# One tile's tables, attention and projections rearranged in a two-block transformer kernel

## The chip, the cores and the metric

The kernel runs on one core of a Trainium2 chip. Its time is the device time of one execution, in microseconds (us). Engines are named as in the profile: PE (TensorE), DVE (VectorE), ACT (ScalarE), POOL (GpSimd), SP (SyncE, which here only issues transfers). Everything is float32.

## The reference, cut to what matters

Sequence 256, width 1024, 16 meta tokens in front. Two blocks follow each other. The first is a mixer and an expert layer:

```python
proj = rms_norm(h, norm1_g) @ w_in
attn = sliding_window_attention(q, k, v, ...)      # head norms of q and k, window 128, sinks, 8 heads
ssm  = s5_ssm(u, ...)                              # 32 groups, 64 complex states, gelu, gate
h = h + concat(rms_norm(attn), rms_norm(ssm)) @ w_out
q = rms_norm(h) @ w_query                          # 8 product-key heads, top 16 of 16384 experts each
h = h + sum over 8*16 experts of gelu(peer_u[idx] . h) * g * peer_v[idx]
```

The second block has an "even" layer (dilated and differential attention) and an "odd" layer (MoBA and NSA attention), each of the form

```python
p = rmsnorm(x, ln) @ w_in          # 8 column chunks: heads, values, gates
x = x + concat(attention_a * silu(gate_0), attention_b * silu(gate_1)) @ w_out
```

## The kernel before, in words

The tokens are cut into two tiles of 128, T = 0 and T = 1 (the meta tokens go with tile 0). The program is written out by hand: each stage is a generator for each engine which emits some instructions and yields, and `steps`, `side_by_side`, `beside`, `paced` and `woven` (lines 219 to 258 and 2038) weave generators into one order. Every engine runs its own instructions in the order in which they were emitted and waits on semaphores. A round is one such yield.

**Mixer, tile 0 (up to about 145 us).** `Tables` (line 688) makes sines and cosines of 16 x 145 angles: DVE makes the angles of the first half (`angles`), ACT the sines (`first_sines`), POOL folds the output matrices (`pool`, line 787, seven operations of 128x512) and then makes the angles of the second half (three operations of 128x1160), and ACT takes an absolute value and the second sines (`last_sines`). Then `ssm(t, 0)` (56 rounds, three for each of 16 steps j and a tail: PE drives, DVE rotates, scans and turns back, PE reads out) is run `beside` a second lane `mixer`, which gets 0.8 rounds for each round of the scan: `project_u`, then `norm1(1)` with `project_qkv(0)`, `last_sines`, `head_norm1(0)` with `project_u1`, `attention1(0)` with `project_qkv(1)`, `mix_attention(0)`. After it come `close_mixer(0)` side by side with `head_norm1(1)`, and half of `query(0)`.

**Expert layer (about 165 to 990 us).** `Peer` gathers 256 times 128 rows of 8 KB (line 1387; 16 experts x 8 heads x 2 tiles) through POOL's queue into 6, then 7, then 8 buffers. In each round n DVE takes the dot products (line 1320), ACT the gelu, the weight and a diagonal matrix (lines 1354 to 1361), and PE two matmuls of two passes each (line 1374), which free the buffer; a quarter of tile 1's rows are added on DVE (line 1300) instead. The first 32 gathers use 6 buffers, since the seventh lies over tile 1's attention data; the rest wait for `attn_ready[1]`. One step of the lane `rest` is emitted per round: the rest of `query(0)`, `attention1(1)` (one head per step; one PSUM bank for turned probabilities, `turn_bank`), `mix_attention(1)`, `ssm(1)`, `close_mixer(1)`, `query(1)`. After round 140 two steps of the second block's tile 0 lane (`ahead`) are added per round.

**Second block.** `Lane` holds a tile's buffers and banks. `project` (line 1649) multiplies eight chunks of weights, 16 matmul instructions each (line 1681), into `banks`: one bank (`pa`), or two where `L.spare` is set (tile 0, until the gathers end). Its generator for ACT evicts each chunk in the round in which PE's last matmul of it was emitted (lines 1704 to 1728). `stream` is the attention. Tile 1's lane (`main`) starts when the gathers are done and runs beside what is left of tile 0's odd layer, which stops before its compression step until `L.done["far"]` is set there. A lane that has sent its output sets `L.done["finished"]`.

**Weights.** A ring of three buffers is filled by SP in the order of use (line 127), a chunk as soon as the chunk three before it is used.

Of the kernel before, what the change touches and what calls it, by code (L numbers as in the profile page):

```python
# [267 lines left out]
def norm1(t, T):  # L268
# [34 lines left out]
    def dve():  # L303
        t.dve.wait_ge(t.constants, 32)
# [124 lines left out]
def head_norm1(t, T):  # L429
# [4 lines left out]
    n = 2 if T == 0 else 1  # L434

# [17 lines left out]
    def dve():  # L453
# [19 lines left out]
        t.dve.tensor_scalar(t.QTt[T][:, :, :], t.PS[2][:, :].rearrange("p (a m) -> p a m", a=4), t.col("qn"), -0.125,  # L473
                            ALU.mult, ALU.mult).then_inc(*placed.add())
        t.dve.wait_ge(*turned.at(2))
        t.dve.tensor_scalar(t.KTt[:, :, T * P:(T + 1) * P], t.PS[3][:, 0:2 * P].rearrange("p (g m) -> p g m", g=2),
                            t.col("kn"), None, ALU.mult).then_inc(*placed.add())
        if T == 0:
            t.dve.tensor_scalar(t.KTt[:, :, SEQ:],
                                t.PS[3][:, 2 * P:2 * P + 2 * META].rearrange("p (g m) -> p g m", g=2),  # L480
                                t.col("kn"), None, ALU.mult).then_inc(*placed.add())
# [3 lines left out]
    def pe():  # L485
# [4 lines left out]
        if T == 1:  # L490
            t.pe.wait_ge(*t.half_added[0])
        for a in range(4):
            ins = t.pe.transpose(t.PS[2][:, a * P:(a + 1) * P], t.qx[:, a * P:(a + 1) * P], t.ident[:, :])
        ins.then_inc(*turned.add())
        t.pe.wait_ge(*normed.at(n + 2))
        for g in range(2):
            ins = t.pe.transpose(t.PS[3][:, g * P:(g + 1) * P], t.kx[:, g].rearrange("p x d -> p (x d)"), t.ident[:, :])
        if T == 0:
            t.pe.wait_ge(*normed.at(n + 3))
            for g in range(2):  # L500
                ins = t.pe.transpose(t.PS[3][:, 2 * P + g * META:2 * P + (g + 1) * META],
# [7 lines left out]
def attention1(t, T):  # L509
# [15 lines left out]
    turn_bank, out, apt = t.PS[2], t.PS[3], t.apt[T]  # L525

    def pe():
# [16 lines left out]
        def turn(i):  # L544
            t.pe.wait_ge(*expd.at(i + 1))
            if i >= 1:
                t.pe.wait_ge(*placed.at(i))
            for e in range(E):
                c = 0
                for n, (k0, k1) in enumerate(kb):  # L550
                    m = (e * (n_k + 1) + n) * P
                    ins = t.pe.transpose(turn_bank[0:k1 - k0, m:m + P], p_at(i, e)[:, c:c + k1 - k0], t.ident[:, :])
                    c += k1 - k0
# [14 lines left out]
        for i in range(NU + 4):  # L568
            if i < NU:
                scores(i)  # L570
            if i >= 4:
                mix(i - 4)
            if 2 <= i <= NU + 1:
                turn(i - 2)
            yield

    def dve():
# [4 lines left out]
        for i in range(NU + 4):  # L582
            if i < NU:
                t.dve.wait_ge(*scored.at(i + 1))
                if i >= R:
                    t.dve.wait_ge(*turned.at(i - R + 1))
                for e, h in enumerate(sets[i]):
                    ins = t.dve.tensor_tensor_reduce(p_at(i, e), s_at(i, e), bias, 1.0, t.nsink[:, h:h + 1], ALU.add,  # L588
                                                     ALU.min, t.amn[:, h:h + 1])
                ins.then_inc(*least.add())  # L590
            if i == NU:
# [13 lines left out]
    def act():  # L605
        for i in range(NU + 4):
            if 3 <= i <= NU + 2:
                n = i - 3
# [3 lines left out]
                of = turn_bank[:, 0:E * (n_k + 1) * P].rearrange("p (e n m) -> p e n m", e=E, m=P)  # L612
# [3 lines left out]
            if 1 <= i <= NU:  # L616
                n = i - 1
# [6 lines left out]
            if i == NU + 1:  # L624
# [63 lines left out]
class Tables:  # L688

    HALF = ST // 2

    def __init__(self, t):
# [4 lines left out]
        self.dts, self.turns, self.sines, self.folded = (t.sem(x) for x in ("t_dts", "t_turns", "t_sines", "t_folded"))  # L699
        t.diagonal, t.folded, t.sines = self.dts.at(3), self.folded.at(1), [self.sines.at(2), self.sines.at(3)]  # L700
# [31 lines left out]
    def angles(self):  # L732

        t, ch = self.t, self.t.dch
        h = slice(0, self.HALF)
        S, C = t.SIN[:, h, :], t.COS[:, h, :]
        ch.step(t.dve.tensor_tensor(S, bc(self.frac[:, h], SPAN + 1), bm(t.col("time"), self.HALF), ALU.mult))
        ch.step(t.dve.tensor_scalar(C, S, ROUND, ROUND, ALU.add, ALU.subtract))
        ch.step(t.dve.tensor_tensor(S, S, C, ALU.subtract))
# [1938 lines left out]
```

## Time and profile before

| | us |
|---|---|
| median of three executions (1281.91 to 1285.24) | 1283.33 |
| the profiled execution: its own time | 1284.34 |
| its span, from first to last instruction | 1282.6 |
| busy PE / DVE / ACT / POOL | 1103.5 / 758.7 / 528.1 / 319.8 |
| first and last gather issued (line 1387) | 164.7, 975.9 |
| tile 0's and tile 1's outputs sent (line 2388), first and last | 1096.1, 1280.3 |

A busy share is an average over stages with different limits, so the profile is read stage by stage. An "x" with a number counts instructions; "idle before" is the engine's idle time ahead of a group, with what ended it.

### The profile page before, as it was taken

The numbers are of one execution on the slowest core, as the hardware profiler recorded it, in microseconds if no ns is written. First come the engines' busy times: TensorE is split into PE (matmuls) and PEld (weight loads), VectorE is DVE, ScalarE is ACT, GpSimd is POOL, SyncE is SP. The second block draws the span as 40 slices with busy tenths as digits, with TensorE's granted clock in tenths as the row PEclk, the third lists the DMA queues.
The fourth block names the chain that finished last, engine by engine and source line by source line (L and its number), as shares of the span: only waits on it lengthen the run. The fifth ranks groups of instructions, "written<-read, shape, count | busy, mean of one in ns | idle before, by whom it ended". The sixth has DMA issues, their size and how long they took to land.

```text
span 1282.6 us, 12167 instructions
## 1 busy us (share of the span) xinstructions
PE 1103.5 (86%) x3770; PEld 585.4 (46%) x3770; DVE 758.7 (59%) x1973; ACT 528.1 (41%) x1381; POOL 319.8 (25%) x302
## 2 busy tenths in 40 slices
PE   5998778888999979986898969898887899988998
PEld 5675534434444434432343434343432644543675
DVE  6564463469999666468775777785566322332343
ACT  4332226844344544344556463555463221212231
POOL 5100022244444333334232234333223000000000
PEclk9989889999999999999899999999898899999988
DMA  7021598789999999999999998999988454545430
GB/s 298 1 99 66 213 389 315 236 293 423 405 362 409 423 422 425 423 422 420 417 426 424 425 399 338 426 422 421 424 313 356 175 205 189 213 197 184 180 131 17
DMA packets 51728, 395.22 MB, mean 308 GB/s; under 512 B 5536, under 2 KB 10400, under 8 KB 11472
## 3 DMA queue, kind: packets, MB, share of 16 engines
q0 software_dynamic: 37536, 270.90, 52.3%
q1 hardware_dynamic: 13552, 122.83, 24.0%
q10 hardware_dynamic: 576, 0.72, 0.2%
q8 instruction: 30, 0.49, 0.2%
q14 instruction: 34, 0.28, 0.1%
HBM read 393.38 MB, written 1.05 MB: 308 GB/s over the span
## 4 chain that ended last, share of the span: by engine, by line
PE 52%; DVE 20%; DMA 12%; ACT 11%; issue 4%; POOL 0%; DVEq 0%; ACTq 0%
PE bank L1681 16%; PE bank L1374 12%; DMA expert_rows<-in_peer_uv,peer_idx 11%; DVE expert_rows L1320 8%; PE bank L1895 3%; PE bank L1928 2%; ACT L1442 2%; PE bank L1087 2%; ACT L1354 2%; PE bank L2079 1%; PE bank L1550 1%; ACT peer_diag L1361 1%; PE bank L1906 1%; PE bank L401 1%; PE bank L1588 1%
## 5 line engine op out<-in xcount | busy, mean ns | idle before, releaser
L1374 PE MATMUL bank<-expert_rows,peer_diag 128*128 128x512 f32 x896 | 452.3, 637 | 95.9 <-ACT peer_diag L1361 94.5
L1387 POOL DMA_INDIRECT expert_rows<-in_peer_uv,peer_idx x256 | 292.8, 1144 | 558.4 <-PE bank L1374 463.5
L1320 DVE CUSTOM_DVE_ANT_0 expert_rows<-expert_rows,HN 128x1024 f32<-128x1024 f32 x256 | 308.8, 1221 | 85.6 <-DMA expert_rows<-in_peer_uv,peer_idx 84.7
L1374 PEld LDWEIGHTS bank<-expert_rows,peer_diag 128*128 128x128 f32 x896 | 168.3, 199 | 311.8 <-issue 159.8
L1681 PE MATMUL bank<-w_ring,b_xt 128*128 128x512 f32 (+1 forms) x576 | 276.7, 604 | 14.0 <-ACT b_sq L1710 11.6
L1354 ACT ACTIVATE peer_dots<-peer_dots 128x1 f32<-128x1 f32 x256 | 51.6, 202 | 302.4 <-DVE peer_dots L1320 301.8
L1681 PEld LDWEIGHTS bank<-w_ring,b_xt 128*128 128x128 f32 x576 | 104.9, 196 | 118.0 <-issue 113.0
L1361 ACT ACTIVATE peer_diag<-ident,peer_dots 128x128 f32<-128x128 f32 x224 | 89.9, 402 | 7.3
L1355 ACT ACTIVATE peer_dots<-peer_dots,peer_ex 128x1 f32<-128x1 f32 x256 | 75.4, 295 | 8.3
L1442 ACT ACT_TABLE_LOAD x53 | 68.0, 1283 | 15.8 <-PE bank L1011 6.2
L2388 POOL DMA_DIRECT2D out<-x_res x4 | 2.2, 559 | 276.9 <-DVE x_res L1608 164.3
L1354 ACT ACT_TABLE_LOAD x47 | 60.3, 1283 | 12.2 <-DVE peer_dots L1320 11.4
L2012 ACT ACTIVATE b_s<-b_s,b_mn 128x128 f32<-128x128 f32 (+3 forms) x96 | 39.1, 419 | 57.8 <-DVE b_mn L1953 57.7
L1087 PE MATMUL bank<-w_ring,xt 128*128 128x512 f32 (+1 forms) x160 | 59.6, 519 | 0.0
L1763 DVE TENSOR_REDUCE b_hs<-b_sq 128x8 f32<-128x512 f32 (+1 forms) x16 | 10.4, 653 | 78.2 <-ACT b_sq L1710 78.2
L1953 DVE CUSTOM_DVE_ANT_0 b_s<-bank,alibi 128x128 f32<-128x128 f32 (+1 forms) x80 | 24.6, 354 | 50.7 <-PE bank L1895 48.8
L1087 PEld LDWEIGHTS bank<-w_ring,xt 128*128 128x128 f32 x160 | 31.3, 197 | 27.6 <-issue 25.8
L1300 DVE SCALAR_TENSOR_TENSOR x_res<-expert_rows,peer_dots,x_res 128x1024 f32<-128x1024 f32 x32 | 41.0, 1281 | 1.5 <-ACT peer_dots L1355 1.4
L1704 ACT ACTIVATE b_raw<-bank,b_ss 128x512 f32<-128x512 f32 (+1 forms) x16 | 10.5, 656 | 65.0 <-PE bank L1681 65.0
L1968 DVE COPY b_pT<-bank 128x512 f32<-128x512 f32 (+2 forms) x28 | 19.2, 687 | 26.0 <-PE bank L1906 13.2
L588 DVE CUSTOM_DVE_ANT_0 as<-bank,window,nsink 128x144 f32<-128x144 f32 (+1 forms) x16 | 6.6, 434 | 38.9 <-PE bank L539 37.0
L1906 PE MATMUL bank<-ident,b_s 128*128 128x128 f32 (+2 forms) x136 | 22.7, 293 | 7.3 <-DVE b_pT L1968 4.7
(355 smaller groups left out, 1284.8 us busy)
## 6 DMA issues: line engine op xcount, KB each, us to landing
w_ring<-in_w_in_e SPq DMA_DIRECT2D x16, 2048.0 KB
w_ring<-in_w_in_o SPq DMA_DIRECT2D x14, 2048.0 KB
w_ring<-in_w_query SPq DMA_DIRECT2D x8, 2048.0 KB
w_ring<-in_w_out SPq DMA_DIRECT2D x4, 2048.0 KB
w_ring<-in_w_out_e SPq DMA_DIRECT2D x4, 2048.0 KB
w_ring<-in_w_out_o SPq DMA_DIRECT2D x4, 2048.0 KB
w_ring<-in_w_in SPq DMA_DIRECT2D x2, 2048.0 KB
expert_rows<-in_peer_uv,peer_idx POOLq DMA_INDIRECT x256, 13.3
```

The costliest lines, as they stand in the source:

```text
L1087: ins = t.pe.matmul(t.PS[4 + u % 2][:, 0:n * P], t.xt[:, k, :], t.w.at(f + i, k, c * P, (c + n) * P), start=k == 0, stop=k == KT - 1)
L1300: engine.scalar_tensor_tensor(x, self.slot(n)[:, D:], self.dots[:, it, at:at + 1], x, ALU.mult, ALU.add).then_inc(*self.added.add())
L1320: t.dve.tensor_tensor_reduce(u, u, t.HN[:, it // PH, :], 1.0, 0.0, ALU.mult, ALU.add, self.dots[:, it, k:k + 1]).then_inc(*self.dotted.add())
L1354: t.ach.step(t.act.activation(one, one, ACT.Gelu))
L1355: t.act.activation(one, one, ACT.Copy, scale=share).then_inc(*self.weighed.add())
L1361: t.act.activation(self.diag[:, d % self.RD, :], t.ident[:, :], ACT.Copy, scale=one).then_inc(*self.diagd.add())
L1374: ins = t.pe.matmul(t.PS[2 * T + c][:, :], self.diag[:, d % self.RD, :], self.slot(n)[:, D + c * 512:D + (c + 1) * 512], start=k == 0, sto ...
L1387: t.pool.indirect_dma_start(self.slot(n), None, t.dram["peer_uv"], bass.IndirectOffsetOnAxis(ap=self.idx[:, it, k:k + 1], axis=0)).then_in ...
L1442: t.act.preload_act_table_set("natural_log_exp_and_others")
L1681: ins = t.pe.matmul(pa[:, 0:n], L.xt[:, k, :], t.w.at(i, k, 0, n), start=k == 0, stop=k == KT - 1)
L1895: ins = t.pe.matmul(L.pb[:, c:c + k.shape[1]], q, k, start=True, stop=True)
L2012: ins = t.act.activation(p, p, ACT.Exp, bias=L.mn[:, column(x, j)], scale=-1.0, **kw)
```

## The change

Several edits, in the order of the file. The tables: the work of `Tables.pool` goes to DVE as two lanes that yield, `fold` (seven operations) and `angles(1)` (four operations, the absolute value among them, which ACT made before), and the lane's stages are regrouped. `norm1(1)` runs with `project_u` instead of `project_qkv(0)`, its PE and DVE parts three rounds late. `head_norm1(1)` runs with `mix_attention(0)` instead of `close_mixer(0)`, in banks 0 and 1 instead of 2 and 3, and waits for tile 0's attention instead of its first output projection. The lane `mixer` gets 1.0 rounds for each round of the scan instead of 0.8. `attention1(1)` has one more step between PE, DVE and ACT and a second bank (6) for turned probabilities; it takes two rounds more. `project` evicts `L.lead` rounds later (3 for tile 0 until the gathers end, else 0). `inherit` gives tile 1's lane tile 0's bank `pt` (bank 5) as a second projection bank in a layer that begins after tile 0 has finished. PE waits for `heads_ready[1]` before the first expert matmul and POOL before the first gather.

```diff
@@ norm1 @@
         if T == 1:
+            for _ in range(3):
+                yield
             t.pe.wait_ge(*t.u_ready.at(4))
...
     def dve():
+        if T == 1:
+            for _ in range(3):
+                yield
@@ head_norm1 @@
+    banks = ((t.PS[2], t.PS[3]), (t.PS[0], t.PS[1]))[T]
...
         if T == 1:
-            t.pe.wait_ge(*t.half_added[0])
+            t.pe.wait_ge(*t.attn_ready[0])
@@ attention1 @@
-    turn_bank, out, apt = t.PS[2], t.PS[3], t.apt[T]
+    turn_banks, out, apt = ((t.PS[2],), (t.PS[2], t.PS[6]))[T], t.PS[3], t.apt[T]
+    TB = len(turn_banks)
+    sums, exps, turns, places, mixes = ((0, 1, 2, 3, 4), (1, 2, 3, 4, 5))[T]
...
-            if i >= 1:
-                t.pe.wait_ge(*placed.at(i))
+            if i >= TB:
+                t.pe.wait_ge(*placed.at(i - TB + 1))
...
-            if i == NU + 3:
+            if i == NU + mixes - 1:
+                yield from T * (None,)
                 t.dve.wait_ge(*sunk.at(2))
@@ Tables @@
-    def angles(self):
+    def angles(self, half):
...
-        h = slice(0, self.HALF)
+        h = slice(half * self.HALF, (half + 1) * self.HALF)
...
-        ch.step(t.dve.tensor_scalar(C, S, ROUND, ROUND, ALU.add, ALU.subtract))
...
+        ch.mark(t.dve.tensor_scalar(C, S, ROUND, ROUND, ALU.add, ALU.subtract))
+        yield
+        ch.wait()
...
     def last_sines(self):
...
-        t.act.wait_ge(*self.folded.at(2))
+        t.act.wait_ge(*self.turns.at(5))
         t.act_set = "sines"
-        h = slice(self.HALF, ST)
-        t.ach.step(t.act.activation(t.COS[:, h, :], t.SIN[:, h, :], ACT.Abs))
-        self.sine(h)
+        self.sine(slice(self.HALF, ST))
...
-    def pool(self):
+    def fold(self):
-        t, ch = self.t, self.t.pch
+        t, ch = self.t, self.t.dch
         w = 2 * SC
-        t.pool.wait_ge(*self.turns.at(4))
-        t.pool.wait_ge(t.late, 64)
-        ch.mark(t.pool.tensor_tensor(t.cpr[:, :, :], t.cr[:, :, :], bc(self.cfr, w), ALU.mult))
+        t.dve.wait_ge(t.late, 64)
+        ch.mark(t.dve.tensor_tensor(t.cpr[:, :, :], t.cr[:, :, :], bc(self.cfr, w), ALU.mult))
+        ch.step(t.dve.tensor_tensor(t.ct[:, :, :], t.ci[:, :, :], bc(self.cfi, w), ALU.mult))
+        ch.mark(t.dve.tensor_tensor(t.cni[:, :, :], t.cr[:, :, :], bc(self.nfi, w), ALU.mult))
+        yield
+        ch.wait()
+        ch.step(t.dve.tensor_tensor(t.cpr[:, :, :], t.cpr[:, :, :], t.ct[:, :, :], ALU.subtract))
+        ch.mark(t.dve.tensor_scalar(t.cnr[:, :, :], t.cpr[:, :, :], -1.0, None, ALU.mult))
+        ch.step(t.dve.tensor_tensor(t.ct[:, :, :], t.ci[:, :, :], bc(self.cfr, w), ALU.mult))
+        t.dve.tensor_tensor(t.cni[:, :, :], t.cni[:, :, :], t.ct[:, :, :], ALU.subtract).then_inc(*self.turns.add())
+        yield
...
@@ Peer.tensor @@
+        t.pe.wait_ge(*t.heads_ready[1])
@@ project, act @@
             if kind == "add":
                 continue
+            for _ in range(L.lead):
+                yield
@@ new, called before turn_x in even_layer and odd_layer @@
+def inherit(L):
+    if L.T == 1 and L.spare is None and "finished" in L.other.done:
+        L.spare, L.free[1] = L.other.pt, L.other.done["x"]
@@ both_blocks @@
-    tables.angles()
+    run(tables.angles(0))
...
-    tables.pool()
     inputs = project_u(t)
     next(inputs)
-    mixer = one_by_one(lambda: inputs, lambda: side_by_side(norm1(t, 1), project_qkv(t, 0)), tables.last_sines,
+    mixer = one_by_one(lambda: side_by_side(inputs, tables.fold(), norm1(t, 1)),
+                       lambda: side_by_side(project_qkv(t, 0), one_by_one(lambda: tables.angles(1), tables.last_sines)),
                        lambda: side_by_side(head_norm1(t, 0), project_u1(t)),
-                       lambda: side_by_side(attention1(t, 0), project_qkv(t, 1)), lambda: mix_attention(t, 0))
+                       lambda: side_by_side(attention1(t, 0), project_qkv(t, 1)),
+                       lambda: side_by_side(mix_attention(t, 0), head_norm1(t, 1)))
...
-    run(beside(ssm(t, 0), mixer, 0.8))
+    run(beside(ssm(t, 0), mixer, 1.0))
     run(mixer)
     t.w.pump(t.sp)
-    run(side_by_side(close_mixer(t, 0), head_norm1(t, 1)))
+    run(close_mixer(t, 0))
...
+    t.pool.wait_ge(*t.heads_ready[1])
     peer.gathers(0, peer.FEW)
```

## Rows read from the trace of the kernel before

**Rows 1.** The page of the profile: DMA share in 40 slices, and the projections' group.

```profile
DMA  7021598789999999999999998999988454545430
...
L1681 PE MATMUL bank<-w_ring,b_xt 128*128 128x512 f32 (+1 forms) x576 | 276.7, 604 | 14.0 <-ACT b_sq L1710 11.6
```

**Rows 2.** Busy time by stage: us, then each engine's busy us and instructions, clock, DMA share, GB/s.

```profile
176.00:285.00 109.00, 89.82 (x302) 46.57 (x304) 53.73 (x141) 69.48 (x157) 26.93 (x26) 0.94 0.81 297
285.00:424.00 139.00, 128.50 (x423) 60.90 (x423) 132.50 (x360) 55.78 (x170) 62.46 (x53) 0.98 0.99 401
...
700.00:976.00 276.00, 231.96 (x650) 110.25 (x649) 190.89 (x462) 144.29 (x375) 97.63 (x83) 0.96 0.97 397
976.00:1128.00 152.00, 134.56 (x528) 77.03 (x527) 54.38 (x154) 37.82 (x111) 3.64 (x5) 0.92 0.55 211
1128.00:1283.00 155.00, 141.59 (x591) 85.95 (x589) 50.79 (x143) 34.44 (x110) 1.08 (x2) 0.93 0.35 138
```

**Rows 3.** Waits of PE, 14 to 165 us: us in total, times, longest.

```profile
PE bank L298 <- ACT HN L288: 4.0, 1, 4.0
...
PE bank L864 <- DMA w_ring<-in_glu_w: 2.2, 1, 2.2
...
PE bank L493 <- issue: 1.9, 1, 1.9
```

**Rows 4.** Timeline, 0 to 60 us: start, duration, instruction, idle before it.

```profile
8.34 1.36 DVE L737 TENSOR_TENSOR sin<-small,cols 128x1160 f32<-128x1160 f32 x1
...
9.73 0.77 DVE L738 TENSOR_SCALAR cos<-sin 128x1160 f32<-128x1160 f32 x1
...
27.93 4.29 POOL L804 TENSOR_SCALAR cos<-sin 128x1160 f32<-128x1160 f32 x1
...
28.14 3.98 DVE L918 TENSOR_TENSOR g<-r,cos 128x256 f32<-128x256 f32 x1
...
38.02 0.42 DVE L918 TENSOR_TENSOR g<-r,cos 128x256 f32<-128x256 f32 x1
```

**Rows 5.** The tile x_res, 0 to 40 us: issue of its second load, landing times.

```profile
L2463 SPq DMA_DIRECT2D x_res<-in_x x1: 4972/4972/4972, 5.3 to 5.3; - x1
...
DMA to landing us min/median/max: 4.0/11.7/19.4
```

**Rows 6.** Timeline, 106 to 165 us: the start of two steps of the scan, one j apart.

```profile
109.24 0.45 DVE L894 TENSOR_TENSOR a<-bank,cos 128x288 f32<-128x288 f32 x1
...
112.01 0.45 DVE L894 TENSOR_TENSOR a<-bank,cos 128x288 f32<-128x288 f32 x1
```

**Rows 7.** Chain of work that ended last, 60 to 145 us: PE's share of one j.

```profile
94.56 0.99 PE bank L855 x8
...
99.30 0.68 PE bank L839 x4
```

**Rows 8.** Timeline, 226 to 262 us: ACT's table load at two ends of one round.

```profile
238.64 1.28 ACT L1442 ACT_TABLE_LOAD   x1
...
243.26 1.28 ACT L1442 ACT_TABLE_LOAD   x1
```

**Rows 9.** Waits of DVE, 176 to 285 us.

```profile
DVE attn L599 <- PE bank L564: 4.7, 1, 4.7
DVE aden L596 <- ACT adsk L627: 4.1, 1, 4.1
```

**Rows 10.** Busy time by 16 us in the stretch of the gathers: its emptiest stretch of DMA.

```profile
760.00:776.00 16.00, 9.87 (x22) 4.52 (x21) 13.29 (x30) 10.13 (x24) 4.23 (x4) 0.79 0.78 295
```

**Rows 11.** Waits of DVE, 600 to 976 us: for tile 0's evicted gates.

```profile
DVE b_gate L1780 <- ACT b_gate L1715: 21.5, 4, 7.0
```

**Rows 12.** Timeline, 936 to 1003 us: the last eviction of tile 0's last projection.

```profile
953.22 0.69 ACT L1714 ACTIVATE b_sq<-bank,b_ss 128x512 f32<-128x512 f32 x1 [1.24 <-PE bank L1681]
```

**Rows 13.** Waits of PE, 1144 to 1283 us.

```profile
PE bank L1681 <- ACT b_sq L1710: 6.2, 4, 1.8
PE bank L1681 <- ACT b_gate L1720: 0.2, 1, 0.2
```

More of the change, by code:

```diff
@@ L496, in pe @@
         for g in range(2):
-            ins = t.pe.transpose(t.PS[3][:, g * P:(g + 1) * P], t.kx[:, g].rearrange("p x d -> p (x d)"), t.ident[:, :])
+            ins = t.pe.transpose(banks[1][:, g * P:(g + 1) * P], t.kx[:, g].rearrange("p x d -> p (x d)"), t.ident[:, :])
         if T == 0:
@@ L500, in pe @@
             for g in range(2):
-                ins = t.pe.transpose(t.PS[3][:, 2 * P + g * META:2 * P + (g + 1) * META],
+                ins = t.pe.transpose(banks[1][:, 2 * P + g * META:2 * P + (g + 1) * META],
                                      t.kxm[:, g].rearrange("p x d -> p (x d)"), t.ident[0:META, 0:META])
@@ L566, in mix @@
             ins.then_inc(*mixed.add())
-        for i in range(NU + 4):
+        for i in range(NU + mixes):
             if i < NU:
                 scores(i)
[L571 to L574, printed above, removed]
+            if i >= mixes:
+                mix(i - mixes)
+            if turns <= i < NU + turns:
+                turn(i - turns)
             yield
@@ L580, in dve @@
             t.dch.step(t.dve.tensor_scalar(t.nsink[:, :], t.row("sinks"), -1.0, None, ALU.mult))
[L582 to L588, printed above, removed]
+        for i in range(NU + mixes):
+            n = i - sums
+            if 0 <= n < NU:
+                t.dve.wait_ge(*scored.at(n + 1))
+                if n >= R:
+                    t.dve.wait_ge(*turned.at(n - R + 1))
+                for e, h in enumerate(sets[n]):
+                    ins = t.dve.tensor_tensor_reduce(p_at(n, e), s_at(n, e), bias, 1.0, t.nsink[:, h:h + 1], ALU.add,
                                                      ALU.min, t.amn[:, h:h + 1])
                 ins.then_inc(*least.add())
-            if i == NU:
+            if n == NU:
                 t.dve.wait_ge(*least.at(NU))
                 t.dve.tensor_tensor(t.adsk[:, :], t.amn[:, :], t.nsink[:, :], ALU.subtract).then_inc(*sunk.add())
-            if i == NU + 3:
+            if i == NU + mixes - 1:
+                yield from T * (None,)
                 t.dve.wait_ge(*sunk.at(2))
@@ L605, in act @@
     def act():
-        for i in range(NU + 4):
-            if 3 <= i <= NU + 2:
-                n = i - 3
+        for i in range(NU + mixes):
+            if places <= i < NU + places:
+                n = i - places
                 t.act.wait_ge(*turned.at(n + 1))
@@ L698, in __init__ @@
         t.mag = self.mag
-        self.dts, self.turns, self.sines, self.folded = (t.sem(x) for x in ("t_dts", "t_turns", "t_sines", "t_folded"))
-        t.diagonal, t.folded, t.sines = self.dts.at(3), self.folded.at(1), [self.sines.at(2), self.sines.at(3)]
+        self.dts, self.turns, self.sines = (t.sem(x) for x in ("t_dts", "t_turns", "t_sines"))
+        t.diagonal, t.folded, t.sines = self.dts.at(3), self.turns.at(4), [self.sines.at(2), self.sines.at(3)]
     def exponents(self):
@@ L2284, in even_layer @@
     outs = [(hd(L.mixed[:, 0:512]), (), None), (L.o3[:, 0:4, :], (), None), (L.o3[:, 4:8, :], (), None)]
+    inherit(L)
     yield from turn_x(L, "ln_e")
@@ L2372, in odd_layer @@
             (hd(tmp), ("sig", t.col("cmp_row")) if T == 0 else ("sig",), (acc, 0))]
+    inherit(L)
     yield from turn_x(L, "ln_o")
```

40 lines of the change are left out of this document (17 added, 23 removed).

## The prediction

> **What bounds the kernel now.** I read the page first, then the busy time by stage, then the waits of PE stage by stage, and the timeline where a wait is worth several us.
>
> The slices show 16 busy DMA engines from about a fifth to two thirds of the span [rows 1]. By stage [rows 2] the kernel has four limits. In the mixer (up to 165 us) PE is the engine that is nearly always busy. From 176 to 285 us, with six row buffers, no engine is full over the stage (PE 90 of 109 us, ACT 69, DVE 54) and DMA stands at 0.81. From 285 to 976 us DMA is full (0.99 and 0.97), and in the first 139 us of it DVE is nearly full as well (132.5). From 976 us on DMA is at 0.55 and then 0.35, and PE is busy 276 of 307 us. So an engine made faster between 285 and 976 us buys nothing but the holes of the DMA; the start of that stretch, and what follows it, count in full, because the bytes are the same and the stretch is only moved.
>
> **The mixer.** PE loses 4.0 us to the normalized rows of tile 1 and 2.2 us to the load of the gate weights, and 1.9 us ahead of the head norm's transposes in the closing stage [rows 3].
>
> *norm1(1) earlier: -4.0 us.* ACT now starts it behind all four evictions of project_u, and PE has nothing else. In the change its ACT part is emitted in the first round. Its input is issued at 5.29 us and lands 19.4 us later, at 24.7 us at the latest [rows 5]; ACT needs some 3 us behind it (an estimate), and PE comes to the transposes only after the last chunk of u, about when POOL's and DVE's rows of [rows 4] end. The 4.0 us are gone if DVE keeps up. ACT's evictions of u now wait behind the landing, but the scan needs the second chunk only at its fifth step.
>
> *The tables on DVE: 0.* DVE gets seven operations of 512 columns and four of 1160. The rows of the first half give 1.36 us for a product of 1160 columns and 0.77 us for the rounding [rows 4]. So angles(1) is 3 x 1.36 + 0.77 = 4.9 us, and the fold, by the share of columns (0.44), 6 x 0.60 + 0.34 = 3.9 us: 8.8 us more. Against it, a turning back takes 3.98 us beside POOL's rounding (4.29 us) and 0.42 us otherwise [rows 4]: 3.6 us back in that one place. The net 5 us lie in a stage in which DVE is not the limit; without that cover they would cost 5 us, and at best the freed contention gives 1.6 us more. I take 0. ACT loses its absolute value, which nobody waits for.
>
> *Gate weights: -2.2 us.* They are loaded when project_u1 ends. Before, it ends at lane round 19, which is scan round 24 at a rate of 0.8, and the gates are due in scan round 27; now it ends in round 20 of 27, so that seven rounds of PE work lie between instead of three.
>
> *The rate of 1.0: +2.5 us.* The lane had 39 rounds, spread over 49 of 56 scan rounds. Now it has 42 and ends with 14 scan rounds left, against 7. A scan step j is three rounds; alone it takes 112.01 - 109.24 = 2.77 us on DVE [rows 6] and 0.99 + 0.68 = 1.67 us on PE [rows 7], so each leaves PE idle for 1.1 us: 14/3 x 1.1 = 5.1 against 7/3 x 1.1 = 2.6. The bounds are 0 (head norm and gates fill it) and 14/3 x 2.77 = 12.9 us (nothing does).
>
> *head_norm1(1) out of the closing stage: -1.9 us* [rows 3]. The reduction and the two products leave DVE's queue there; the transposes go to banks 0 and 1, which the lane's attention and projection have left. In the mixer they hide in the idle time of the rate's term. Not below 0.
>
> Mixer: -4.0 - 2.2 + 2.5 - 1.9 = **-5.6 us** (bounds -9 and 0).
>
> **Six buffers, 176 to 285 us: -3.5 us.** In the rounds of attention1(1), ACT's table loads come 243.26 - 238.64 = 4.62 us apart and ACT has no gap: two loads, an exponential, the gelu, a diagonal and the turned copy [rows 8]. So the second bank and the step between engines buy nothing in these rounds, though PE stops waiting for ACT's copy. What they buy is at the end: DVE stands 4.1 us for the sinks' exponential and 4.7 us for the last mix [rows 9], with row products queued behind both. With one more step both are done when DVE comes. I take 3.5 of the 8.8 us, because ACT is full until the first of these waits ends and cannot use more; the ends are 0 and 8.8. The two added rounds hold no work. They move mix_attention(1) and all that follows two rounds later, query(1) too: its first scores are then emitted in the round in which DVE asks for them, a stall of at most one such round (4.6 us) under full DMA, hidden by seven buffers. The new waits of PE and POOL for heads_ready[1] are met long before.
>
> **The gathers, 285 to 976 us: -1.5 us.** Tile 0's evictions make ACT and DVE wait for PE: 21.5 us on DVE in four gates alone [rows 11], and what is queued behind is the experts' products and weights. Later evictions shorten this, but only the holes count: the emptiest 16 us have a DMA share of 0.78, 3.5 us lost [rows 10]. I take somewhat less than half of such a hole; the ends are 0 and 3.5.
>
> Does the lag push tile 0's work out of the stretch? A chunk has eight rounds of matmuls, and the longest path of ACT grows from 3 to 6 rounds, so it doesn't add up over chunks; some 3 rounds at each place where the attention waits for heads, 6 to 9 steps in all. The last eviction of tile 0's last projection is at 953.2 us [rows 12], and a gather takes 276 / 83 = 3.3 us [rows 2]; so about 7 rounds, 14 steps, are left until the stretch ends. Cost 0.
>
> **The tail: -6.2 us.** Tile 0's output goes out from 1096 us on, before tile 1's odd layer starts at about 1144 us, so inherit works for that layer and not for the even one. From there PE waits four times, 6.2 us in all, for an eviction (copy and square of the same bank), and 0.2 us for a gate [rows 13]. With two banks an eviction (6.2 / 4 = 1.6 us) lies beside the next chunk (16 x 276.7 / 576 = 7.7 us of PE [rows 1]). Next late would be the weights, but DMA is at 0.35 there. Bounds -6.4 and 0.
>
> **Sum.** -5.6 - 3.5 - 1.5 - 6.2 = -16.8 us. The profiled execution has a time of 1284.34 us (span 1282.6), 1.0 us above the median: 1267.5 us on its base, **1267 us** against the median of 1283.3, which is 1.3% less. With every term at its best end (-9 - 8.8 - 3.5 - 6.4) it would be 1256 us.
>
> **Rivals.** About 0.3% (4 us) is what a measurement can tell from no change.
>
> *The mixer gives nothing* (0.2): DVE, with 8.8 us more and a last stretch of 14 scan rounds to itself, becomes its bound, and the first gather comes no earlier. For it: the scan alone is slower on DVE than on PE [rows 6, 7]. Against it: the waits of [rows 3] are PE's, and DVE is far from full up to 165 us. 1267 + 5.6 = 1273 us.
>
> *The shift is swallowed* (0.1): between 285 and 424 us DVE is busy for 132.5 of 139 us [rows 2]; if it sets the pace there rather than DMA, an earlier start of the gathers could end in a longer wait of the DMA. Then only tail and holes are left: 1284.3 - 7.7 - 1.0 = 1276 us.
>
> *The clock* (0.1). The last stage has a granted clock of 0.93 of the 2.4 GHz level [rows 2]. If it fell to 0.89 with another rhythm of matmuls, PE's 141.6 us would become 148.0 and the tail's gain would be gone: 1273 us. The Trainium skill (TensorE: Matmul & The Clock Gate, section "A second HAM failure mode: psum-queue depth-cycling") reports a kernel that cycled through PSUM banks and paused so often between groups that its clock oscillated; by that rule a second bank is itself the risk. Against it: here it is the single bank that has the pauses, and the second takes them away.
>
> *Slower* (0.05): the lag in project does add up. With 3 rounds for each of 16 chunks tile 0 is 48 steps late, 34 more than the slack of 14, and each has two projection instructions, 2 x 276.7 / 576 = 0.96 us of PE [rows 1], which then lie in the tail: 33 us, less 16.8, 1299 us. It decides from about 32 steps of lateness on (14 + 16.8 / 0.96). Against it stands the count of 6 rounds in 8.
>
> **Numbers.** The forecast as summed has 0.55. The range takes in its best end and, above, the rivals that are still faster: 1255 to 1279 us. Faster by over 0.3%: nearly all of the forecast and of the first three rivals, 0.87; within 0.3% 0.07, for a swallowed shift together with a weaker tail; slower 0.06.
>
> **What would show it.** PE's wait for HN gone and the wait for the gate weights gone; the turning back at 0.42 us throughout; POOL without products; the first gather some 5 to 6 us before 164.7 us; rounds of attention1(1) still 4.6 us with ACT full; the last gather 9 to 10 us earlier; no PE wait for an eviction in tile 1's odd layer, and still the other 11.6 - 6.2 = 5.4 us of them before it. I am wrong if the first gather is not earlier, if the stretch from first to last gather grows, or if tile 0's last eviction comes after the last gather.

## The result and the profile after

The changed kernel takes 1249.95 us (median of four executions, 1245.49 to 1258.2) against 1284.28 us before (four executions): ratio 0.9742, 95% interval 0.9688 to 0.9795. Measured again beside other kernels it took 1253.82 us against 1287.03 us, 0.9740 (0.9713 to 0.9766). The change is worth about 33 us, twice the 16.8 us that were forecast. One execution of all those below, of the changed kernel with its attention as before, fell into a slow state (2632.47 us at a granted clock of 0.431) and is left out of the figures.

The page of the changed kernel: its first line, the DMA share in 40 slices and the projections' group [rows 1].

```profile
span 1243.8 us, 12163 instructions
...
DMA  7041699689999999999999999999999454555530
...
L1693 PE MATMUL bank<-w_ring,b_xt 128*128 128x512 f32 (+1 forms) x576 | 278.3, 608 | 7.7 <-ACT b_sq L1724 5.4
```

The row of 9s ends earlier and has no 8s left in its second half; PE's idle time ahead of the projections fell from 14.0 to 7.7 us.

Busy time by stage of the changed kernel, cut at its own first gather (154) and last gather (950), against [rows 2]. Columns: stretch, us, then PE, PEld, DVE, ACT and POOL busy, granted clock, DMA share, GB/s.

```profile
154.00:264.00 110.00, 95.28 (x310) 49.86 (x311) 59.26 (x170) 71.70 (x158) 31.47 (x31) 0.91 0.86 326
264.00:404.00 140.00, 130.48 (x417) 61.36 (x415) 130.30 (x356) 56.13 (x171) 64.46 (x53) 0.98 0.99 392
404.00:680.00 276.00, 237.81 (x612) 109.65 (x612) 183.30 (x442) 128.67 (x341) 100.58 (x89) 0.94 1.01 420
680.00:950.00 270.00, 233.75 (x655) 110.78 (x654) 192.69 (x463) 149.86 (x381) 95.13 (x84) 0.96 1.00 416
950.00:1102.00 152.00, 133.71 (x534) 75.24 (x533) 56.12 (x157) 39.06 (x113) 3.66 (x5) 0.94 0.55 212
1102.00:1243.00 141.00, 135.40 (x584) 82.55 (x582) 48.91 (x141) 33.22 (x108) 1.08 (x2) 0.95 0.38 146
```

The stretch up to the last gather moved 416 GB/s where it had moved 397 [rows 2]; the last stage, up to the end of the span, is 12.8 us shorter (154.6 to 141.8) with 6.2 us less PE work in it. In the two profiled executions the span fell from 1282.6 to 1243.8 us: 10.8 us ahead of the first gather (164.7 to 153.9), 15.2 us between first and last gather (811.2 to 796.0), 12.8 us behind it (306.7 to 293.9).

PE's waits in the mixer of the changed kernel (14 to 154 us), the counterpart of [rows 3], where the waits for HN, for the gate weights and ahead of the head norm are gone:

```profile
PE bank L866 <- DVE g L929: 5.1, 5, 1.7
PE bank L1014 <- DVE mT L953: 3.0, 1, 3.0
PE bank L300 <- ACT uT L342: 1.3, 1, 1.3
```

Behind the last gather, PE's waits of the changed kernel from 950 to 1102 us, where tile 1 still has one bank; from 1102 us on, with two, PE waits for no eviction, against 6.2 us in [rows 13].

```profile
PE bank L1693 <- ACT b_sq L1724: 5.4, 4, 1.5
```

### The profile page after: what moved, and what is told of

It is laid out like the page before. It is cut to its first block, busy times and chain, and to the rows that moved or that the text cites. A ratio compares the mean times of both kernels' runs of the same rounds, so it can differ in the third digit from the quotient of the medians.

```text
span 1243.8 us, 12163 instructions
## 1 busy us (share of the span) xinstructions
PE 1095.5 (88%) x3770; PEld 580.7 (47%) x3770; DVE 760.2 (61%) x1984; ACT 527.1 (42%) x1380; POOL 303.3 (24%) x292
## 4 chain that ended last, share of the span: by engine, by line
PE 48%; DVE 19%; DMA 16%; ACT 12%; issue 4%; SPq 0%; POOL 0%; DVEq 0%; ACTq 0%
DMA expert_rows<-in_peer_uv,peer_idx 15%; PE bank L1693 14%; PE bank L1386 13%; DVE expert_rows L1331 7%; ACT L1454 3%; ACT L1365 2%; PE bank L1915 2%; PE bank L1948 2%; PE bank L1098 2%; DMA x_res<-in_x 2%; PE bank L1014 1%; PE bank L2099 1%; DVE r L914 1%; ACT peer_dots L1366 1%; PE bank L1926 1%
## 5 line engine op out<-in xcount | busy, mean ns | idle before, releaser
L1454 ACT ACT_TABLE_LOAD x53 | 68.0, 1283 | 22.6 <-PE bank L1022 8.2
L1365 ACT ACT_TABLE_LOAD x48 | 61.6, 1283 | 12.2 <-DVE peer_dots L1331 11.4
L966 POOL COPY last<-r 128x2 f32<-128x2 f32 x16 | 3.0, 188 | 107.4 <-DVE r L914 107.4
L1926 PEld LDWEIGHTS bank<-ident,b_s 128*128 128x128 f32 (+2 forms) x136 | 17.0, 145 | 24.8 <-issue 11.0
## 6 DMA issues: line engine op xcount, KB each, us to landing
w_ring<-in_w_in_e SPq DMA_DIRECT2D x16, 2048.0 KB, 11.6
```

The lines of the kernel that those rows point to most:

```text
L1365: t.ach.step(t.act.activation(one, one, ACT.Gelu))
L1454: t.act.preload_act_table_set("natural_log_exp_and_others")
L1926: ins = t.pe.transpose(L.pt[0:x.m, turns(x, j, n)], scores(x, j)[:, n * P:n * P + x.m], t.ident[:, :])
```

## The experiments

**One part at a time.** The change has four independent parts. Each was put alone into the kernel before. Below, the ratio is to the kernel before timed beside it (medians 1283.85 to 1287.03 us), and "less" is that ratio turned into us.

The mixer alone:

```diff
-    tables.pool()
...
+    mixer = one_by_one(lambda: side_by_side(inputs, tables.fold(), norm1(t, 1)),
...
+                       lambda: side_by_side(mix_attention(t, 0), head_norm1(t, 1)))
...
+    run(beside(ssm(t, 0), mixer, 1.0))
```

> The kernel before with the edits of the mixer alone (tables on DVE, norm1(1) and head_norm1(1) moved, rate 1.0, the two waits for heads_ready[1]). Theory A (the parts add up, and the mixer's is the 10.8 us by which the first gather moved): the first gather at about 154 us, the whole 8 to 11 us shorter than before, 1274 to 1276 us. Theory B (the forecast's own terms): 5 to 6 us, 1279 us. Theory C (the mixer's gain is swallowed between 285 and 424 us, where DVE is full): first gather at 154 us, but under 3 us in the end.

Measured: 1279.9 us, ratio 0.9958 (0.9938 to 0.9979), 5.4 us less: the forecast's own figure, theory B.

The attention of tile 1 alone:

```diff
-    turn_bank, out, apt = t.PS[2], t.PS[3], t.apt[T]
+    turn_banks, out, apt = ((t.PS[2],), (t.PS[2], t.PS[6]))[T], t.PS[3], t.apt[T]
+    sums, exps, turns, places, mixes = ((0, 1, 2, 3, 4), (1, 2, 3, 4, 5))[T]
```

> The kernel before with only the step between engines and the second bank of attention1(1). Forecast: 3.5 us, 1281 us, rounds of 4.6 us as before. Theory A: 4 to 8 us, since gathers 12 to 40 gained up to that much beside the mixer's shift. Rival: 0 to 1 us, since ACT is full in these rounds, and the gathers catch up later under full DMA.

Measured: 1280.9 us, 0.9962 (0.9938 to 0.9986), 4.9 us less. ACT's table loads in this kernel still come a round of 4.62 us apart, as forecast:

```profile
214.65 1.28 ACT L1447 ACT_TABLE_LOAD   x1
...
219.27 1.28 ACT L1447 ACT_TABLE_LOAD   x1
```

The later evictions alone:

```diff
+            for _ in range(L.lead):
+                yield
             ps = banks[j % nb]
```

> The kernel before with only the evictions of tile 0 made three rounds later until the gathers end. Forecast: 1.5 us, 1283 us. Theory A: 8 to 10 us, 1275 us, with the hole of the DMA between 936 and 968 us gone and the last gather 8 to 10 us earlier. Rival: 0, and the shift after gather 210 comes from the earlier start alone.

Measured: 1267.3 us, 0.9875 (0.9845 to 0.9905), 16.1 us less. More than theory A had, ten times the forecast of 1.5 us.

The second bank for tile 1 alone:

```diff
+def inherit(L):
+    if L.T == 1 and L.spare is None and "finished" in L.other.done:
+        L.spare, L.free[1] = L.other.pt, L.other.done["x"]
```

> The kernel before with only inherit (bank 5 as a second bank in tile 1's odd layer). Forecast: 6.2 us, 1278 us, no PE wait for an eviction after 1144 us. Theory A, by the 12.8 us of the tail: 6.2 us of waits and some 6 us of clock, because PE's pauses are what lowers its clock: 12 us, 1272 us, with the granted clock of the last 140 us at 0.96 or more against 0.93. Rival: 6 us, and the clock of the tail differs by chance from kernel to kernel.

Measured: 1274.83 us, 0.9929 (0.9899 to 0.9959), 9.1 us less (5.3 to 13.0). The forecast's 6.2 lies in that interval and so does theory A's 12, but theory A's reason fails: the granted clock of the last 140 us is 0.93, as before.

**The later evictions.** The sum of the four (35.5 us) is near the whole 33, so the surplus is in one term. First it was taken out of the changed kernel:

```diff
-            for _ in range(L.lead):
-                yield
             ps = banks[j % nb]
```

> The changed kernel with the evictions where they were before. If the parts add up, it loses what they gave alone: 14 to 18 us, 1264 to 1268 us, and the stretch from first to last gather is about 811 us again instead of 796. If the parts share a gain, it loses under 10 us.

Measured: 1266.27 us, 0.9877 (0.9855 to 0.9900). The three other parts together give 15.8 us (12.8 to 18.6), where the forecast had 15.3. From first to last gather it is 808.1 us.

Where the 16 us come from shows in the DMA rate. Busy time by stretches of the kernel before:

```profile
424.00:700.00 276.00, 233.85 (x598) 105.95 (x597) 180.01 (x433) 133.40 (x346) 98.07 (x89) 0.96 1.01 423
...
753.00:785.00 32.00, 24.12 (x65) 11.99 (x64) 26.59 (x63) 15.22 (x38) 11.54 (x10) 0.87 0.84 315
785.00:817.00 32.00, 29.06 (x73) 12.85 (x72) 23.25 (x50) 12.37 (x37) 13.80 (x12) 1.00 1.01 423
913.00:945.00 32.00, 28.59 (x91) 14.20 (x90) 17.26 (x50) 19.69 (x51) 6.80 (x8) 0.91 0.98 391
945.00:976.00 31.00, 24.99 (x70) 11.17 (x70) 20.75 (x32) 17.60 (x54) 18.08 (x15) 1.00 0.87 335
```

A full stretch moves 423 GB/s. Against that the three poor ones lose (1 - 315/423) x 32 = 8.2, 2.4 and 6.4 us, 17 us in all; and 397 instead of 423 GB/s over the whole 276 us [rows 2] is 276 x (1 - 397/423) = 17 us too. The same two places with the later evictions alone:

```profile
747.00:779.00 32.00, 25.57 (x63) 11.18 (x62) 26.28 (x62) 13.56 (x36) 11.20 (x10) 0.89 0.90 364
...
907.00:939.00 32.00, 29.97 (x104) 15.85 (x104) 19.45 (x53) 23.86 (x64) 10.76 (x9) 0.95 1.01 423
```

The first hole is down to 4.5 us and the second nearly gone: in the last 31.5 us up to the last gather the rate is 404 GB/s, 1.4 us lost. The timeline of the kernel before shows what precedes the second (start, duration, instruction, idle before it):

```profile
931.73 0.69 ACT L1714 ACTIVATE b_sq<-bank,b_ss 128x512 f32<-128x512 f32 x1 [7.93 <-PE bank L1681]
...
933.02 0.69 DVE L1780 SCALAR_TENSOR_TENSOR b_gate<-b_sq,b_gate 128x512 f32<-128x512 f32 x1 [7.02 <-ACT b_gate L1715]
...
935.91 3.47 PE L1374 MATMUL bank<-expert_rows,peer_diag 128*128 128x512 f32 x4 [3.41 <-ACT peer_diag L1361]
...
936.33 0.94 POOL L1387 DMA_INDIRECT expert_rows<-in_peer_uv,peer_idx  x1 [6.46 <-DVE x_res L1300]
...
954.52 0.69 DVE L1780 SCALAR_TENSOR_TENSOR b_gate<-b_sq,b_gate 128x512 f32<-128x512 f32 x1 [6.45 <-ACT b_gate L1715]
```

ACT comes to the eviction of a gate chunk while PE still has expert matmuls and attention ahead of the chunk's last piece, and stands 7.9 us. DVE stands behind it for the gate, with the products of gathered rows in its queue; then PE has no diagonal, and POOL no free buffer. Some 21 us later DVE stands again, 6.45 us, for the next gate; the larger part of the loss (6.4 of 8.8 us) lies around and behind this second stand. With the later evictions (that part alone) the instructions of the first stand have no idle time before them:

```profile
917.60 0.67 ACT L1716 ACTIVATE b_sq<-bank,b_ss 128x512 f32<-128x512 f32 x1
...
920.63 0.68 DVE L1782 SCALAR_TENSOR_TENSOR b_gate<-b_sq,b_gate 128x512 f32<-128x512 f32 x1
```

The stand for the next gate is still there (5.4 us, at 940.86 us), and hardly costs anything by itself.

One round instead of three:

```diff
-            for _ in range(L.lead):
+            for _ in range(L.lead // 3):
```

> The kernel before, tile 0's evictions one round later instead of three. Theory Q (ACT stands in its queue ahead of an eviction until PE has reached that chunk, 47.8 us in all between 600 and 976 us before and 1.8 us with three rounds; DVE waits behind it, and so buffers come free late): one round of emission is a third of the way, a gain of 4 to 8 us, 1278 to 1282 us, ACT's waits for the bank 20 to 35 us. Rival S (any lag works, since it is the order within a round that matters): the full 14 to 16 us, 1268 to 1271 us.

Measured: 1266.8 us, 0.9881 (0.9854 to 0.9909), 15.3 us less; rival S. Yet most of the waits are still there. DVE's three waits behind ACT from 600 us to the last gather, before (its third is in [rows 11]):

```profile
DVE b_hs L1763 <- ACT b_sq L1710: 34.5, 8, 6.5
...
DVE b_raw L1769 <- ACT b_rs L1739: 13.6, 5, 4.2
```

and with one round:

```profile
DVE b_hs L1765 <- ACT b_sq L1712: 32.3, 8, 7.2
...
DVE b_gate L1782 <- ACT b_gate L1717: 14.6, 4, 6.1
DVE b_raw L1771 <- ACT b_rs L1741: 7.1, 5, 2.5
```

69.6 us became 54.0 (26.0 with three rounds). The sum of such waits is thus no measure of the cost. That what counts is whether the waits are long and close enough to empty the buffers fits the holes, but no run shows it by itself.

Six rounds:

```diff
-            for _ in range(L.lead):
+            for _ in range(2 * L.lead):
```

> The kernel before, tile 0's evictions six rounds later instead of three. Theory Q: ACT's waits for PE are gone with three rounds, so nothing more is to be had; DMA at 420 GB/s throughout gives at most 5 us more; against it PE may wait for its banks and the attention for its heads: within 5 us of three rounds, 1264 to 1273 us. Rival F (what helps is that the lane of tile 0 is later as a whole, and leaves DVE to the gathers): another 5 to 10 us less in the gathers, and a longer tail.

Measured: 1281.37 us, 0.9961 (0.9939 to 0.9983), 5 us less than before and outside what either theory said. From first to last gather the profiled execution takes 816.0 us, more than before; ACT's waits for PE's bank are gone, but the hole that was at 753 to 785 us has grown:

```profile
756.00:800.00 44.00, 34.19 (x84) 16.01 (x83) 31.57 (x70) 21.09 (x56) 14.51 (x13) 0.79 0.85 312
```

Only DVE's part of each eviction late, ACT's in its old place:

```diff
+            for _ in range(L.lead):
+                yield
             t.dve.wait_ge(*taken.at(got))
             if kind in ("heads", "kv"):
```

> The kernel before with ACT's evictions where they were and only DVE's part of each (head sums, gates) three rounds later. It tells whose queue held the buffers. Theory Q in its ACT form: ACT still waits 40 to 50 us for PE's bank, diagonals come late, gain under 4 us, 1282 to 1286 us. Theory Q in its DVE form (the 69.6 us which DVE waits for ACT's squares, gates and roots are what holds up the products of the gathered rows): most of the gain, 10 us or more, 1268 to 1275 us, though ACT still waits.

Measured: 1275.48 us, 0.9927 (0.9904 to 0.9951), 9.4 us less, between the two forms. ACT's own waits for the bank stay at 41.5 us. By the medians more than half of the gain is thus DVE's queue, and the rest needs ACT's. In the profile the second hole is gone with this edit (0.2 us lost in the last 80 us of the gathers) and the first is not (7.7 us).

Only the gates late, and only the heads and key-values late:

```diff
+            for _ in range(L.lead if kind == "gate" else 0):
+                yield
```

> The kernel before, with only the evictions of tile 0's gate chunks made three rounds later. Before, the DMA loses some 8 us around gather 186 and some 8 us around gather 239; at the second, ACT and DVE stand 7.9 and 7.0 us for a gate chunk of which PE has matmuls left, with the products of the rows behind it. Theory H (each hole is such a stand, and the second is one of the gates): the second hole is gone, the first stays, 1276 us, stretch from first to last gather 803 to 806 us. Rival: the gates are nothing by themselves, since one stand moves to the next chunk: under 3 us.

```diff
+            for _ in range(L.lead if kind in ("heads", "kv") else 0):
+                yield
```

> The counterpart: only the evictions of tile 0's heads and key-value chunks three rounds later. Theory H: the second hole stays (8 us), and the first, around gather 186, goes by 0 to 4 us: 1280 to 1284 us. Rival (the whole gain comes of the heads, whose square, sum and root wait for each other on two engines): 1268 to 1271 us.

Measured: gates 1274.25 us, 0.9917 (0.9885 to 0.9948); heads 1282.09 us, 0.9964 (0.9939 to 0.9989). The totals are those of theory H, the holes are not: with late gates the second hole only shrank (from 8.6 to 4.9 us), and the first shrank too (8.2 to 5.7), while with late heads the second nearly went and the first nearly doubled, to 14.9 us:

```profile
754.00:794.00 40.00, 28.77 (x71) 14.06 (x71) 32.65 (x79) 22.95 (x57) 11.45 (x12) 0.77 0.75 265
```

The timelines say why the first of these runs is no clean test. With late gates ACT no longer waits for PE at a gate, but DVE's product is emitted right behind ACT's eviction, and ACT comes to that with exponentials and table loads of other heads ahead. So DVE stands for the same gate as long as before:

```profile
938.43 0.69 DVE L1782 SCALAR_TENSOR_TENSOR b_gate<-b_sq,b_gate 128x512 f32<-128x512 f32 x1 [6.73 <-ACT b_gate L1717]
```

With late heads a stand of ACT for PE, with 6.2 us of DVE's behind it, lies just ahead of the hole that grew; the longest ahead of that hole in the kernel before is 5.1 us:

```profile
746.62 0.69 ACT L1716 ACTIVATE b_sq<-bank,b_ss 128x512 f32<-128x512 f32 x1 [9.43 <-PE bank L1681]
```

Over the last 80 us or so of the gathers DVE stands for gates 7.0 and 6.5 us in the kernel before (8.6 us of DMA lost) and 6.7 and 3.5 with late gates (4.9 lost). The kernels with one stand of 5.4 to 7.5 us there and none other above 3 us (one, three or six rounds, DVE's part late, late heads) lose 0.2 to 3.5 us. That two long stands close together are what empties the buffers is a reading of these profiles; no run varied it alone. In the profiled stretch the two lags together do more (11.6 us) than the one (6.2) and the other (-2.4); in the timed medians they simply add up (10.7 and 4.6 against 16.1).

**The other parts, in the changed kernel.** The rate of 0.8 again:

```diff
-    run(beside(ssm(t, 0), mixer, 1.0))
+    run(beside(ssm(t, 0), mixer, 0.8))
```

> The changed kernel with the lane's rate at 0.8 again. By the forecast's rate term (+2.5 us for the rate of 1.0) it would be 2.5 us faster, 1247 us, but the gate weights would be waited for again (2.2 us): 1247 to 1250 us. Rival: the lane then has a rest to run after the scan, PE-bound by itself, and it is slower by 1 to 4 us.

Measured: 1259.64 us, 0.9784 (0.9752 to 0.9817), against 0.9740 of the changed kernel. The gate weights are waited for again, in this kernel from 14 to 164 us:

```profile
PE bank L875 <- DMA w_ring<-in_glu_w: 3.8, 1, 3.8
...
PE bank L875 <- ACT zT L989: 1.6, 1, 1.6
...
PE bank L866 <- DVE g L929: 1.1, 2, 0.6
```

Less the 0.4 us for zT in the changed kernel that is 5.0 us more, and 4.0 less behind DVE. In the profiled executions the whole distance is clock: the first gather comes 9.0 us later than in the second profile of the changed kernel, and 15.3 against 5.1 us are lost to the clock ahead of it (see below). The timed distance is 5.7 us with an uncertainty of about 5, so that the rate's own worth is not shown.

Attention as before in the changed kernel:

```diff
-    turn_banks, out, apt = ((t.PS[2],), (t.PS[2], t.PS[6]))[T], t.PS[3], t.apt[T]
-    sums, exps, turns, places, mixes = ((0, 1, 2, 3, 4), (1, 2, 3, 4, 5))[T]
+    turn_bank, out, apt = t.PS[2], t.PS[3], t.apt[T]
```

> The changed kernel with attention1(1) as before (one bank, one step less). If the part is worth what the waits of the six-buffer stage say, the gathers 33 to 40 come 2 to 4 us later after the first one and the whole loses 3 to 4 us, 1253 to 1254 us. Rival (an earlier start of the full stretch is swallowed): 1250 us as before.

Measured: 1258.37 us (median of five), 0.9788 (0.9750 to 0.9826), 6 us slower than the changed kernel, with an uncertainty of about 6 us; gather 33 (counted from 0) comes 119.8 us after the first, against 117.7.

Four kernels side by side: the changed kernel, its variant with one round of lag, with the tables on POOL, with `norm1(1)` in its old place.

> The changed kernel once more, unchanged, beside the next three. If the parts measured alone add up (mixer 5, attention 5, evictions 16, second bank 9 us) it is at 1249 to 1251 us. If they share some of their gains it is at 1252 to 1256 us. In its profile only the clock should differ from the first one: the start of the first gather between 153 and 160 us and the tail between 293 and 299 us.

```diff
-            for _ in range(L.lead):
+            for _ in range(L.lead // 3):
```

> The changed kernel with tile 0's evictions one round later instead of three. If any small lag does it: within 3 us of the changed kernel. If the wait that is left (ACT stood 26 us for PE's banks with one round, 48 us with none, 2 us with three) counts: 5 to 8 us slower.

```diff
-    mixer = one_by_one(lambda: side_by_side(inputs, tables.fold(), norm1(t, 1)),
+    tables.pool()
+    mixer = one_by_one(lambda: side_by_side(inputs, norm1(t, 1)),
```

> The changed kernel with the tables' fold and the angles of the second half on POOL as before. Forecast: 0, since DVE's 5 us more are covered: within 2 us of the changed kernel, with one turning back at 4 us beside POOL's rounding again. Rival T (freed contention and an earlier second half of the sines are part of the mixer's gain): first gather 2 to 4 us later and the whole slower by as much.

```diff
-    mixer = one_by_one(lambda: side_by_side(inputs, tables.fold(), norm1(t, 1)),
+    mixer = one_by_one(lambda: side_by_side(inputs, tables.fold()),
-                       lambda: side_by_side(project_qkv(t, 0), one_by_one(lambda: tables.angles(1), tables.last_sines)),
+                       lambda: side_by_side(norm1(t, 1), project_qkv(t, 0), one_by_one(lambda: tables.angles(1), tables.last_sines)),
```

> The changed kernel with norm1(1) in its old place beside project_qkv(0). Forecast: PE waits again for the normalized rows of tile 1, 4.0 us, and the first gather and the whole come 3 to 4 us later. Rival: only 1 to 2 us, since the changed kernel waits 1.3 us there for ACT anyway and the lane has slack at a rate of 1.0.

Measured: 1253.82 us (0.9740), 1247.65 us (0.9696, interval 0.9669 to 0.9722), 1252.81 us (0.9741, 0.9713 to 0.9769) and 1255.55 us (0.9762, 0.9734 to 0.9789). The place of the tables makes no difference that can be seen (1 us, with an uncertainty of about 5): with them on POOL the first gather comes 0 to 2 us later, the lost clock taken off, and the stretch to the last gather is 3 to 5 us shorter. `norm1(1)` is worth some 2 us by the medians, which is within the noise: its wait is back, in this kernel as

```profile
PE bank L298 <- ACT HN L288: 4.0, 1, 4.0
```

but the 1.3 us at L300 and 1.5 of the 5.1 us behind DVE go with it. One round of lag in place of three gives 6 us more, with intervals that just overlap (0.9713 and 0.9722): the lowest ratio of all versions. It is not shown that the lag does it: the mean granted clock of its five executions is 0.956 against 0.946 for the changed kernel, and the two profiled executions took the same time (1251.67 and 1251.0 us).

**The stages of all profiled executions.** The first gather, the stretch from first to last gather and the tail behind it, in us; "lost" is length times (1 - granted clock), added up over windows of 6 us, from 12 us on for the first stage. Taking it off a stage is an estimate: it supposes that all of the stage waits for PE.

| kernel | first gather | lost | first to last | tail | lost |
|---|---|---|---|---|---|
| before | 164.7 | 10.3 | 811.2 | 306.7 | 22.2 |
| attention alone | 159.1 | 6.8 | 812.4 | 305.0 | 20.2 |
| second bank alone | 159.8 | 8.5 | 811.9 | 299.0 | 22.3 |
| evictions alone, 3 rounds | 158.3 | 6.8 | 800.2 | 305.7 | 20.5 |
| 1 round | 160.2 | 8.5 | 802.9 | 304.2 | 19.8 |
| 6 rounds | 163.8 | 10.2 | 816.0 | 301.3 | 20.4 |
| DVE's part late | 163.1 | 11.9 | 803.5 | 307.3 | 20.5 |
| gates late | 164.1 | 8.5 | 805.6 | 302.8 | 17.1 |
| heads late | 165.2 | 10.3 | 814.2 | 301.3 | 17.0 |
| mixer alone | 157.4 | 8.5 | 811.8 | 309.3 | 25.6 |
| changed, evictions as before | 157.1 | 8.6 | 808.1 | 297.4 | 20.5 |
| changed, attention as before | 159.0 | 11.9 | 797.6 | 297.7 | 18.8 |
| changed, rate 0.8 | 163.5 | 15.3 | 797.6 | 297.6 | 20.4 |
| changed | 153.9 | 3.5 | 796.0 | 293.9 | 15.3 |
| changed, again | 154.5 | 5.1 | 797.7 | 297.1 | 17.1 |
| changed, 1 round | 159.4 | 11.9 | 793.6 | 296.9 | 18.8 |
| changed, tables on POOL | 160.7 | 10.2 | 792.7 | 297.8 | 19.8 |
| changed, norm1(1) back | 158.5 | 8.5 | 796.1 | 298.3 | 20.5 |

## Why the prediction was right and wrong

The sign was right, and three of the four terms agree in size with what was timed; the total does not, 1267 us with a range down to 1255 against 1250 measured, because of the term for the gathers.

**The mixer, -5.6 forecast.** Right in size. The first nine kernels of the table have the old mixer: first gather at 162.0 us on average, 152.9 with the lost clock taken off. The six with the whole new one (tables on DVE, rate 1.0 and `norm1(1)` early) average 156.9 and 148.6: 5.1 and 4.3 us less; timed 5.4 (2.7 to 8.0). By its steps: the tables cost 0 within the noise. The gate weights' wait is gone, and its price at a rate of 0.8 is even 5.0 us; against it stand 4.0 us behind DVE in the scan's end, so that by these waits the rate term was too small (2.5) and the weights' term too small (2.2), and the two still cancel: in part luck. `norm1(1)` was over-valued: 4.0 us of wait, 2 to 3 us in the time. The bounds of -9 and 0 don't follow from the prediction's own terms, which give -8.1 (-9.7 with the freed contention) and, with a rate term of 12.9, +4.8.

**The six-buffer stage, -3.5 forecast.** Near in size, wrong in its way. Gather 33 came 121.5 us after the first with the old attention and 118.2 with the new one alone, 3.3 us less. But the waits that were to go are there. DVE's waits from 160 to 275 us in the changed kernel:

```profile
DVE as L598 <- PE bank L547: 13.3, 3, 10.3
...
DVE attn L610 <- PE bank L573: 6.0, 1, 6.0
DVE aden L607 <- ACT adsk L638: 6.0, 1, 6.0
```

They were 4.7 and 4.1 [rows 9]. What fell is DVE's wait for the scores (the first row, and 5.8 us at another matmul), which in the kernel before was, from 176 to 285 us,

```profile
DVE as L588 <- PE bank L539: 26.0, 7, 12.8
```

No profile shows the 3 us reaching the end: the whole stretch to the last gather is no shorter, neither alone (812.4 against 811.2 to 811.9 us) nor in the changed kernel (796.0 and 797.7 us, against 797.6 with the old attention), which is the rival of the swallowed shift in small. Timed, the part is worth 4.9 us alone (1.8 to 8.0) and 6 in the changed kernel (0 to 12). Where that time is saved stays open, so the agreement with -3.5 may be luck.

**The gathers, -1.5 forecast, 16 measured (12 to 20).** This is the step that failed: "only the holes count: the emptiest 16 us have a DMA share of 0.78, 3.5 us lost". It took one window for the stage's loss and then less than half of it. The stage's own row had the answer, 397 GB/s [rows 2] beside the 423 of a full stretch: 17 us were lost, in two holes of about 8 us each, and 11.6 of them came back. Even the emptiest window was priced too low by its share: by its rate [rows 10] it lost 16 x (1 - 295/423) = 4.8 us. The upper bound of 3.5 us was therefore no bound, and with it the low end of the range fell. The waits named, 21.5 us in four gates, were a part of the cause only: DVE waits 69.6 us behind ACT in all, and the gates alone late gave 10.7 of the 16 us. The profiled stretch shows 11.6 us of the 16 (811.8 on average to 800.2); where the others lie was not settled. The clock may have a part in it: it averages 0.953 over the timed executions with late evictions alone and 0.948 before. But taken out of the changed kernel the part costs 17.6 us in the time and 10 to 12 in the stretch, at an equal clock (0.947 and 0.946).

**The tail, -6.2 forecast.** Right to the wait: no eviction is waited for in tile 1's odd layer, and 5.4 us are left before it. With one bank the tails of the table average 304.8 us, with two 297.3; without the lost clock 284.5 and 278.0, 6.5 us less (timed 9.1, 5.3 to 13.0).

**The rivals.** The mixer that gives nothing and the slower case by an adding lag both fell: tile 0's last gate is evicted at 930.5 us, 19.5 us ahead of the last gather, against 22.7 before [rows 12]. The clock as a rival fell as well: the lost clock of the tails is 20.4 us on average with one bank and 19.3 with two, 1.1 us apart where single tails differ by up to 10 (15.3 to 25.6). The Trainium skill (TensorE: Matmul & The Clock Gate, section "A second HAM failure mode: psum-queue depth-cycling") tells of a kernel whose clock oscillated while it cycled through PSUM banks; taken as a rule, that would have the second bank raise the loss. These traces don't bear it out: it is no higher with two.

**What stays open.** Why six rounds, or late heads alone, widen the hole near 755 us, where tile 0 goes from its even to its odd layer, was not tried further; the 9.4 us stand of ACT ahead of it with late heads is the nearest thing in the traces. That one round does better than three in the changed kernel rests on one comparison, in which the clock differs too.

## What to carry to other kernels

Where a stage is to run at the DMA's full rate, measure its loss as its length times (1 - its rate / the rate of a full stage), not by its emptiest window, and do it before asking which wait causes it. In a kernel whose engines take their work in emitted order, an eviction emitted with the last matmul can make two queues stand, here ACT for 7.9 us and DVE for 7.0. One round between them was enough here (15.3 us against 16.1 with three), and six lost most of the gain (5.0). Look at the second queue too: a lag for ACT alone does not keep DVE from standing behind it. Change such an order by small steps and time each, since the holes move together.

## What was not expected of the hardware

Programs that are the same up to the first gather reached it between 158.3 and 165.2 us (nine kernels), and part of this follows the granted clock: 6.8 to 11.9 us are lost there to stretches at 1.2 instead of 2.4 GHz, and taking them off leaves 151.2 to 155.6 us, a spread of 4.4 instead of 6.9 us. Of the 38.8 us between the two profiled executions, 6.8 in the mixer and 6.9 in the tail are such differences (10.3 to 3.5 and 22.2 to 15.3), and no edit is known to cause them: the changed kernel's second profile has 5.1 and 17.1. So a single profile of each kernel can mislead by some ten us; the timed executions of the kernel before alone range from 1278.13 to 1294.03 us.

Between first and last gather the lost clock matters far less: in the kernel before and the three with one other part alone it is 30.6 to 46.2 us, and the stretches agree within 1.2 us (811.2 to 812.4). Yet that stretch has a scatter of its own from small shifts of the order: the kernels with evictions three rounds late range from 792.7 to 800.2 us, and the first hole from 1.5 us (tables on POOL) to 5.1 (the changed kernel, second profile).
